# Near and far products of a gated recurrence, made by GpSimd in place of VectorE

## What is computed

```python
def step(s, xs):                       # a chunk of tokens
    qc, kc, gc, vc = xs
    a = jnp.cumsum(gc, axis=2)         # gc: log of the forget gate
    diff = a[:, :, :, None, :] - a[:, :, None, :, :]
    decay = jnp.exp(jnp.where(causal[:, :, None], diff, -jnp.inf))
    scores = jnp.sum(qc[:, :, :, None, :] * kc[:, :, None, :, :] * decay, axis=-1)
    o = jnp.einsum('bhts,bhsv->bhtv', scores, vc) + jnp.einsum('bhtk,bhkv->bhtv', qc * jnp.exp(a), s)
    a_last = a[:, :, -1:, :]
    s_new = jnp.exp(a_last[:, :, 0, :, None]) * s + jnp.einsum('bhsk,bhsv->bhkv', kc * jnp.exp(a_last - a), vc)
    return s_new, o
```

## Time and profile before

| | us |
|---|---|
| median of 3 runs | 3965.97 |
| lowest and highest | 3959.08, 3971.05 |
| span of the profiled execution | 3950.7 |
| recurrence, layer 0 | about 402 to 551 |
| recurrence, layer 1 | about 1340 to 1477 |

### The profile page before, as it was taken

One profiled execution on the slowest core, in us unless ns is written; L12 is line 12 of the kernel. 1 busy time (PEld: TensorE's weight loads), 2 busy tenths in 40 slices (PEclk: granted clock), 3 DMA queues, 4 the chain that ended last, 5 costly groups with the idle time before them and its releaser, 6 DMA issues.

```text
span 3950.7 us, 52215 instructions
## 1 busy us (share of the span) xinstructions
PE 3628.5 (92%) x19934; PEld 2784.4 (70%) x19934; DVE 2203.3 (56%) x3277; ACT 1589.9 (40%) x2690; POOL 304.0 (8%) x398
## 2 busy tenths in 40 slices
PE   8998797999999687999999998999999999889998
PEld 7886465666788445456878766787877878667877
DVE  7866855897785784237762346665233332654332
ACT  3335744898423662113222336322233222453222
POOL 0110001110111002001210000111000001000001
PEclk9999568999999758999999999999999999999999
DMA  7551013998455005997773310575323223312222
GB/s 278 175 170 65 2 54 107 347 373 312 173 195 161 1 34 213 409 406 261 267 240 104 101 59 12 186 232 197 105 81 128 96 94 104 134 33 91 93 94 75
DMA packets 164958, 618.35 MB, mean 157 GB/s; under 512 B 18540, under 2 KB 20117, under 8 KB 163581
## 3 DMA queue, kind: packets, MB, share of 16 engines
q1 hardware_dynamic: 114928, 420.58, 29.6%
q0 software_dynamic: 45568, 166.75, 12.8%
q10 hardware_dynamic: 4238, 27.90, 1.8%
HBM read 595.95 MB, written 16.31 MB: 155 GB/s over the span
## 4 chain that ended last, share of the span: by engine, by line
PE 81%; DVE 8%; ACT 5%; DMA 4%; issue 2%; SPq 0%; ACTq 0%; POOL 0%; DVEq 0%; POOLq 0%
PE psum L2500 23%; PE psum L2513 12%; PE psum L843 12%; PE psum L928 5%; PE psum L995 4%; PE psum L2108 4%; DMA ring<-wtile 3%; PE psum L772 3%; PE psum L2339 2%; PE psum L1212 1%; PE psum L2127 1%; PE psum L2358 1%; PE psum L1222 1%; PE psum L780 1%; DVE spare L1318 1%
## 5 line engine op out<-in xcount | busy, mean ns | idle before, releaser
L796 ACT CAST small_r<-ring 128x1024 fp32r<-128x1024 f32 x263 | 275.0, 1048 | 1070.6 <-PE psum L843 336.6
L800 DVE TENSOR_TENSOR ring_r<-ring,small_r 128x1024 fp32r<-128x1024 f32 x264 | 322.8, 1225 | 677.4 <-ACT small_r L796 677.1
L796 ACT CAST PB_r<-ring 128x1024 fp32r<-128x1024 f32 x247 | 255.8, 1049 | 544.2 <-PE psum L2500 326.8
L800 DVE TENSOR_TENSOR ring_r<-ring,PB_r 128x1024 fp32r<-128x1024 f32 x248 | 299.5, 1222 | 247.8 <-ACT PB_r L796 247.4
L2500 PE MATMUL psum<-H_r,ring_r 128*128 128x512 f32 x1344 | 336.3, 392 | 0.0
L2500 PE MATMUL psum<-H_r,small_r 128*128 128x512 f32 x1344 | 326.9, 395 | 0.0
L2500 PE MATMUL psum<-H_r,PB_r 128*128 128x512 f32 x1344 | 318.7, 390 | 0.0
L2500 PEld LDWEIGHTS psum<-H_r,small_r 128*128 128x128 f32 x1344 | 252.4, 188 | 61.1
L2500 PEld LDWEIGHTS psum<-H_r,ring_r 128*128 128x128 f32 x1344 | 252.3, 188 | 55.9
L2500 PEld LDWEIGHTS psum<-H_r,PB_r 128*128 128x128 f32 x1344 | 252.4, 188 | 53.3
L843 PE MATMUL psum<-H_r,small_r 128*128 128x512 f32 (+1 forms) x1040 | 275.2, 368 | 0.1
(11 more groups left out here) (445 smaller groups left out, 6589.7 us busy)
## 6 DMA issues: line engine op xcount, KB each, us to landing
ring<-wtile SPq DMA_DIRECT2D x776, 512.0 KB, 5.3
spare<-wmod POOLq DMA_DIRECT2D x97, 512.0 KB, 4.8
H<-wmod POOLq DMA_DIRECT2D x48, 512.0 KB, 4.5
PB<-wmod POOLq DMA_DIRECT2D x48, 512.0 KB, 4.4
X<-wmod POOLq DMA_DIRECT2D x47, 512.0 KB, 4.9
PB<-wahead POOLq DMA_DIRECT2D x16, 512.0 KB, 7.5
h_rows<-PB POOLq DMA_DIRECT2D x10, 512.0 KB, 4.5
PB<-wmod SPq DMA_DIRECT2D x4, 1024.0 KB, 15.5
```

Of the source, the lines that this page charges most:

```text
L796: copy(high(j), slot(g0 + j)).then_inc(high_ready.sem, 1)
L800: nc.vector.tensor_tensor(low(g0 + j), slot(g0 + j), high(j).bitcast(F32), ALU.subtract).then_inc(low_ready.sem, 1)
```

## The change

`near_product` and `far_product` (four products for each piece, 28 a layer, 56 in all) leave VectorE's list. GpSimd gets a list for this stage with the same products in the same order of pieces: for each piece it waits for the key (`gate_sig` or `gate_bound`), then for the near decay, does the two near products, waits for the far decay, does the two far products and counts `cell_ready`. VectorE's last level product of a piece now counts a new semaphore, `levels_ready`, and TensorE waits for both at each cell's start. Nothing else moves.

```diff
--- before.py
+++ after.py
@@ -291,6 +291,7 @@
         out_squared, out_scale, out_scaled, out_turned = sig("out_squared"), sig("out_scale"), sig("out_scaled"), sig("out_turned")
         out_bounded = sig("out_bounded")
         expo_ready, decay_ready, cell_ready = sig("expo_ready"), sig("decay_ready"), sig("cell_ready")
+        levels_ready = sig("levels_ready")
         prod_ready, hid_split = sig("prod_ready"), sig("hid_split")
         gate_log, gate_low, gate_key, gate_sig = sig("gate_log"), sig("gate_low"), sig("gate_key"), sig("gate_sig")
         gate_bound, gate_full, scan_ready = sig("gate_bound"), sig("gate_full"), sig("scan_ready")
@@ -1447,7 +1448,7 @@
             b_gl, b_gw, b_gk, b_sc = (z.reserve(NPIECE) for z in (gate_log, gate_low, gate_key, scan_ready))
             b_gs = gate_sig.reserve(NPIECE)
             b_gb, b_gf = (z.reserve(NPIECE) for z in (gate_bound, gate_full)) if l else (0, 0)
-            b_ex, b_de, b_ce = expo_ready.reserve(4 * NPIECE), decay_ready.reserve(5 * NPIECE), cell_ready.reserve(NPIECE)
+            b_ex, b_de, b_ce, b_lv = expo_ready.reserve(4 * NPIECE), decay_ready.reserve(5 * NPIECE), cell_ready.reserve(NPIECE), levels_ready.reserve(NPIECE)
             b_sr, b_bc, b_pr, b_or, b_oc = (z.reserve(nw) for z in (scores_ready, between_copied, probs_ready, out_ready, out_copied))
             b_kt, b_kc, b_su, b_st = (z.reserve(nl) for z in (probsT_ready, probsT_copied, sums_ready, state_ready))
             b_cl = between_cleared.reserve(2)
@@ -1475,8 +1476,10 @@
                 def scores(u):
                     c, v, ch, d, i = units[u]
                     if (c, v) == (0, 0):
+                        eng.wait_ge(levels_ready.sem, b_lv + 1)
                         eng.wait_ge(cell_ready.sem, b_ce + 1)
                     if (c, v) == (0, 2) or c and v == 0:
+                        eng.wait_ge(levels_ready.sem, b_lv + c + 2)
                         eng.wait_ge(cell_ready.sem, b_ce + c + 2)
                     if wanted[u]:
                         x = upto_w[u]
@@ -1772,21 +1775,9 @@
                         eng.wait_ge(gate_sig.sem, b_gs + k + 1)
                     eng.wait_ge(decay_ready.sem, b_de + 5 * k + m + 1)
                     nc.vector.tensor_tensor(side(lv, m, 1 - d), side(lv, m, 1 - d), side(query(k), m, 1 - d), ALU.mult)
-                    nc.vector.tensor_tensor(k_side, k_side, side(piece(kk(c), k), m, d), ALU.mult)
-
-                def near_product(k):
-                    c = of(k)
-                    q, key = piece(qd(c), k), piece(kd(c), k)
-                    eng.wait_ge(decay_ready.sem, b_de + 5 * k + 4)
-                    nc.vector.tensor_tensor(q, q, query(k), ALU.mult)
-                    nc.vector.tensor_tensor(key, key, piece(kk(c), k), ALU.mult)
-
-                def far_product(k):
-                    c = of(k)
-                    q, key = piece(qs(c), k), piece(ks(c), k)
-                    eng.wait_ge(decay_ready.sem, b_de + 5 * k + 5)
-                    nc.vector.tensor_tensor(q, q, query(k), ALU.mult)
-                    nc.vector.tensor_tensor(key, key, piece(kk(c), k), ALU.mult).then_inc(cell_ready.sem, 1)
+                    ins = nc.vector.tensor_tensor(k_side, k_side, side(piece(kk(c), k), m, d), ALU.mult)
+                    if m == 2:
+                        ins.then_inc(levels_ready.sem, 1)
 
                 def masked(u):
                     if not wanted[u]:
@@ -1846,8 +1837,6 @@
                 low_log(1)
                 for m in range(3):
                     level_product(0, m)
-                near_product(0)
-                far_product(0)
                 if l:
                     bounds(1)
                 running(1)
@@ -1867,8 +1856,6 @@
                     if (c, v) == (0, 1):
                         for m in range(3):
                             level_product(1, m)
-                        near_product(1)
-                        far_product(1)
                         if l:
                             bounds(2)
                     if (c, v) == (0, 2):
@@ -1887,11 +1874,9 @@
                         level_product(k, 1)
                     if v == (4 if c == 0 else 3) and near:
                         level_product(k, 2)
-                        near_product(k)
                     if v == (5 if c == 0 else 4) and near:
                         if far and l:
                             bounds(k + 1)
-                        far_product(k)
                     if v == 5 and far:
                         running(k + 1)
                     if (c, v) in HEAD_APPLY:
@@ -1905,7 +1890,16 @@
                 tile_low(4)
                 head_apply(2)
                 tile_low(5)
-            stage(tensor=ten, scalar=sca, vector=vec)
+            def poo(eng):
+                for k in range(NPIECE):
+                    c = of(k)
+                    eng.wait_ge(*((gate_bound.sem, b_gb + k + 1) if l else (gate_sig.sem, b_gs + k + 1)))
+                    for at, (q, key) in ((4, (qd(c), kd(c))), (5, (qs(c), ks(c)))):
+                        eng.wait_ge(decay_ready.sem, b_de + 5 * k + at)
+                        nc.gpsimd.tensor_tensor(piece(q, k), piece(q, k), query(k), ALU.mult)
+                        ins = nc.gpsimd.tensor_tensor(piece(key, k), piece(key, k), piece(kk(c), k), ALU.mult)
+                    ins.then_inc(cell_ready.sem, 1)
+            stage(tensor=ten, scalar=sca, vector=vec, gpsimd=poo)
             return normed, weights, order_k, close
 
         class Routing:
```

## The result

The changed kernel takes 3988.04 us (median of 5 runs, 3979.32 to 3999.17) against 3961.16 us for the kernel before (5 runs, 3944.03 to 3971.05). The ratio is 1.0077, with a 95% interval of 1.0051 to 1.0103: slower by about 27 us (20 to 41 by the interval), where 27.9 us was forecast.

The account below looks back on a forecast made before the run. VectorE was taken to pace layer 1's stage, with little to spare in layer 0. Layer 0's 14.1 and layer 1's 13.8 us gave +27.9: 3978.6 on the span, 3993.9 with 15.3 around it; range 3963 to 4012.

Parts of the forecast that it names:

- The sign and the mechanism: Both layers' recurrences: slower, as GpSimd products and VectorE's two-input or `tensor_scalar` instructions exclude each other; +27.9 us, chance 0.68.
- Where the holds fall: One layer 1 cell: holds of 1.8, 1.3, 1.0 and 1.3 us on VectorE, 5.4 us against 3.5 us freed.
- The middle cells: Cells 2 to 4 of each layer: later by 1.7 us each in layer 0, 2.0 us each in layer 1.
- The starts: Start of each layer's stage: first pieces +1.6 and +0.5, second pieces +2.8 each, cell 1 +3.5 and +2.5 us.
- the level products end before the last far product: Each cell's start: level products end before the far key product, so the new wait on `levels_ready` costs nothing by itself.
- a wait for `levels_ready` at a cell's start: Profile after, TensorE at the cells' starts: waits for `levels_ready` there would show the forecast wrong; no size given.
- the waits for GpSimd: Profile after: TensorE waiting for GpSimd at each cell's start would show the forecast right; no size given.
- The last cell: Cell 5, made while VectorE has 5 us to spare: products still end late, +1.1 us layer 0, +2.0 us layer 1.
- The one-way hold: Rival: GpSimd waits for VectorE but not the reverse; net about 0, 3966 us, chance 0.11.
- nothing is held at all: Rival: no mutual hold, GpSimd ends a piece 7.4 us after the near decay; -14 us, 3952 us, chance 0.06.
- masks and state updates are held too: Rival: everything of VectorE is held, nothing overlaps GpSimd's 7.4 us; +50 us, 4016 us, chance 0.08.
- the change finds its room: Rival: holds fall in idle time and waits more often than placed; 0 to +12 us, about 3972 us, chance 0.07.

Follow-up runs that it names:

- last-piece kernel: The changed kernel with only the last piece of each layer made by GpSimd, all others on VectorE; ratio to before 1.0005 (0.9989 to 1.0020).
- idle products: The kernel before, plus GpSimd products of the same number and shapes on tiles that nobody reads; ratio to before 1.0131 (1.0107 to 1.0154).
- short memsets: The changed kernel with each GpSimd query product replaced by three memsets and each key product by two; ratio to before 0.9985 (0.9968 to 1.0003).
- the long ones: The changed kernel with each GpSimd product replaced by three memsets of the same tile; ratio to before 1.0022 (1.0007 to 1.0038).

## Why the prediction was right, and where its parts were off

**The sign and the mechanism** were right. The holds exist in both directions, on instructions with two inputs in SBUF (and, where GpSimd's products were put beside them, on `tensor_scalar` and a small copy with one); masks and state updates are free of them; both recurrences carry the loss, +26.7 us against 27.9. Where the holds fall was partly wrong. I had placed them on `low_log`, the level products, `bounds` and the scan; they fell on `low_log` and the level products alone, since GpSimd got its turns sooner than I placed them. That they sum to 5.8 us in the cell shown, and to 5.4 in my placing, is in part luck.

**The middle cells** were charged too little. I gave 3 x 1.7 us for layer 0 and 3 x 2.0 for layer 1; they cost 2.5, 3.1, 3.6 and 3.7, 2.8, 2.6, 18.3 us in place of 11.1. In layer 1 ScalarE's `bounded` shows behind the holds in some cells. The step that failed is the one that looked for the wait at the cell's start. TensorE waits in the middle of the cell, 1.40 and 0.95 us in the cell shown of layer 0 and 4.4 us in layer 1's, for masks that stand in VectorE's queue behind held level products. The products on GpSimd end at 473.08, while TensorE still works on the cell before until 475.

**The starts** were charged too much: 1.6 + 0.5 for the first pieces (measured 0.9 + 0.8) and 2.8 + 3.5 + 2.8 + 2.5 = 11.6 for what leads to cell 1 (measured 3.7 + 2.4 = 6.1). I had assumed that VectorE's back-to-back products keep GpSimd out until they are through. They don't: the two take turns, so GpSimd works from the moment when its decay lands, and ends 1.3 us ahead of the last level product in layer 0's first cell. So the step that the level products end before the last far product, by which the wait for `levels_ready` costs nothing, was wrong too. I had named a wait for `levels_ready` at a cell's start as a sign that I was wrong, and there it was; the waits for GpSimd that I had named as a sign of being right are absent.

**The last cell** cost 0.0 and 0.6 us where I charged 1.1 and 2.0. The spare time of VectorE took it, and the last-piece kernel says the same. (In layer 1 the clock had risen ahead of this start before the change and not after it, so even the 0.6 may be the clock's.)

So 7.2 us too little in the middle cells and 8.4 us too much at the starts and the last cells cancel. That the sum is closer than its parts is luck. What lies around the span was 1.8 us in the profiled run of the changed kernel (3991.48 against 3989.7), not 15.3. A run of the kernel before with the same span as the profiled one, 3950.7, took 3952.5 us, so the profiled run was a faster one than the median.

**The rivals.** The one-way hold is excluded by the idle products (+44.0 us). Its net of about 0 was near what the short memsets gave (-4.5 us), which is the case without those holds. That nothing is held at all falls with it. That masks and state updates are held too is excluded by their durations, 0.44 and 0.27 us on average over all 60 and 48 of them, as before. That the change finds its room is excluded by +26.7 us.

## What to carry to other kernels

Before moving an elementwise product to GpSimd to relieve VectorE, look at what VectorE does at that time. If it runs instructions with two inputs in SBUF, each GpSimd product of 1.81 us held it here for up to 1.6 us and freed 0.87, and moving half of the products cost half of the loss, whichever half it was. `tensor_scalar` and even a small copy were held too. Two cases were milder here: products made while VectorE had time to spare cost nothing (and gained nothing), and GpSimd instructions that only write held no two-input instruction, though the long ones ended late and cost 8 us. That a move of either kind pays isn't shown. And in a profile, an engine that has fewer instructions but more busy time may be held by another: compare the durations of instructions that weren't changed.

## What was not expected of the hardware

- VectorE and GpSimd took turns, one instruction each, in every stretch shown where both had such work waiting: GpSimd products of 2.12 us one behind the other, each with a VectorE product of 384 columns ahead of it. A busy VectorE queue didn't keep GpSimd out.
- The hold counts as busy time of the held instruction (0.55 us becomes 2.16), so a view of waits doesn't show it.
- TensorE's granted clock is 0.50, the 1.2 GHz level, through a stretch in which it is busy for 20 us of 20, and rises to 1.00 near the stage's end at a moment that differs by tens of us between kernels whose cells start alike (153 us after layer 0's start before, 119 us with the last piece alone, where TensorE was busy for 8.00 us of the 8 up to 523 us). In measures across that moment this was worth some 8 us.
